# Writing the high and the low parts of three mixed weights in one operation each, in a Strassen-style fp32 matrix product

## The reference, cut to what matters

```python
for i in range(DEPTH):                      # DEPTH = 2
    x = x + token_mixer_i(_rmsnorm(x, g_i)) # attention, then short convolution
    x = x + _swiglu(_rmsnorm(x, f_i), w_gate[i], w_up[i], w_down[i])

def _swiglu(h, w_gate, w_up, w_down):
    return (jax.nn.silu(h @ w_gate) * (h @ w_up)) @ w_down
```

## Time and profile before

| what | value |
| --- | --- |
| time, median of 3 runs | 2097.96 us (2097.86 to 2098.32) |
| span of the profiled execution, first to last instruction | 2096.4 us |
| mean granted TensorE clock over the span | 0.999 of full speed |
| busy: TensorE matmul / weight load / DVE / ACT / POOL | 2081.3 / 1729.7 / 1725.3 / 1177.2 / 118.3 us |
| read from HBM | 429.12 MB, 206 GB/s over the span |

### The profile page before, as it was taken

One profiled execution on the slowest core, in us unless ns is written; L12 is line 12 of the kernel. 1 busy time (PEld: TensorE's weight loads), 2 busy tenths in 40 slices (PEclk: granted clock), 3 DMA queues, 4 the chain that ended last, 5 costly groups with the idle time before them and its releaser, 6 DMA issues.

```text
span 2096.4 us, 28772 instructions
## 1 busy us (share of the span) xinstructions
PE 2081.3 (99%) x9675; PEld 1729.7 (83%) x9675; DVE 1725.3 (82%) x1968; ACT 1177.2 (56%) x1428; POOL 118.3 (6%) x131
## 2 busy tenths in 40 slices
PE   8999999999999999999999999999999999999999
PEld 7888878788888888888888888888888888888887
DVE  5887757999999997876788877579999999978666
ACT  5456555665566564554465555466655665645443
POOL 0001000001000000000000000000010000000000
PEclk9999999999999999999999999999999999999999
DMA  7555456777777777667667666567777777767674
GB/s 230 152 145 152 158 171 192 223 224 227 228 226 220 231 219 215 216 202 215 211 196 211 204 203 196 190 196 222 224 226 229 225 221 230 221 213 216 204 220 147
DMA packets 251616, 432.33 MB, mean 206 GB/s; under 512 B 16912, under 2 KB 58000, under 8 KB 251536
## 3 DMA queue, kind: packets, MB, share of 16 engines
q1 hardware_dynamic: 233824, 399.23, 58.8%
q0 software_dynamic: 16848, 30.68, 8.7%
q10 hardware_dynamic: 864, 1.37, 0.2%
HBM read 429.12 MB, written 2.10 MB: 206 GB/s over the span
## 4 chain that ended last, share of the span: by engine, by line
PE 96%; DVE 2%; ACT 1%; issue 1%; DMA 0%; ACTq 0%; DVEq 0%; SPq 0%
PE ps L774 24%; PE ps L776 24%; PE ps L775 24%; PE ps L520 6%; PE ps L551 4%; PE ps L549 4%; PE ps L550 4%; PE ps L525 3%; PE ps L584 2%; DVE w_lo L1393 1%; PE ps L702 0%; PE ps L640 0%; ACT w_hi L1006 0%; PE ps L711 0%; PE ps L692 0%
## 5 line engine op out<-in xcount | busy, mean ns | idle before, releaser
L1393 DVE TENSOR_TENSOR w_lo<-stage,w_hi 128x1024 fp32r<-128x1024 f32 x748 | 902.3, 1222 | 232.4 <-ACT w_hi L1006 228.4
L1006 ACT ACTIVATE w_hi<-stage 128x1024 fp32r<-128x1024 f32 x748 | 772.7, 1055 | 536.6 <-PE ps L776 365.5
L774 PE MATMUL ps<-w_hi,xs 128*128 128x512 f32 x1122 | 439.4, 392 | 0.3
L776 PE MATMUL ps<-w_hi,xs 128*128 128x512 f32 x1122 | 437.0, 389 | 0.0
L775 PE MATMUL ps<-w_lo,xs 128*128 128x512 f32 x1122 | 436.6, 389 | 0.0
L774 PEld LDWEIGHTS ps<-w_hi,xs 128*128 128x128 f32 x1122 | 210.6, 188 | 44.3 <-DVE gated L1699 1.1
L776 PEld LDWEIGHTS ps<-w_hi,xs 128*128 128x128 f32 x1122 | 210.6, 188 | 44.1
L775 PEld LDWEIGHTS ps<-w_lo,xs 128*128 128x128 f32 x1122 | 210.7, 188 | 42.9
L774 PE MATMUL ps<-w_hi,hs 128*128 128x512 f32 x584 | 227.6, 390 | 0.0
L776 PE MATMUL ps<-w_hi,hs 128*128 128x512 f32 x584 | 227.2, 389 | 0.0
L775 PE MATMUL ps<-w_lo,hs 128*128 128x512 f32 x584 | 227.2, 389 | 0.0
(11 more groups left out here) (226 smaller groups left out, 2824.7 us busy)
## 6 DMA issues: line engine op xcount, KB each, us to landing
stage<-in_w_gate SPq DMA_DIRECT2D x176, 512.0 KB, 4.0
stage<-in_w_up SPq DMA_DIRECT2D x176, 512.0 KB, 4.9
stage<-in_w_down SPq DMA_DIRECT2D x176, 512.0 KB, 4.9
stage<-in_conv_w_in SPq DMA_DIRECT2D x96, 512.0 KB, 4.8
stage<-in_attn_w_in SPq DMA_DIRECT2D x48, 512.0 KB, 3.8
stage<-in_w_gate POOLq DMA_DIRECT2D x86, 256.0 KB, 5.6
stage<-in_attn_w_out SPq DMA_DIRECT2D x32, 512.0 KB, 4.8
stage<-in_conv_w_out SPq DMA_DIRECT2D x32, 512.0 KB, 4.8
```

The costliest lines, as they stand in the source:

```text
L774: pe.matmul(ps[:, bank, :], hi, b_hi, start=start, stop=False)
L776: return pe.matmul(ps[:, bank, :], lo, b_hi, start=False, stop=stop)
L1006: nc.scalar.activation(w_hi[:, j % RING, :], stage[:, at, :], ACT.Copy).then_inc(hi_done, 1)
L1393: tt(w_lo[:, p, :], stage[:, stage_at(first + j), :], f32(w_hi[:, p, :]), ALU.subtract).then_inc(lo_done, 1)
```

## The change

ACT writes the high parts of all three mixed weights in one operation of 1536 elements a partition, and DVE writes their low parts in one. Both `t_high` and `t_ready` rise once for a mixed pair instead of twice. TensorE waits for `t_ready` once, ahead of P6. ACT's early wait (for `t_raw[2]` and for P6 of the pair before) is gone, and only the wait for all of `t_raw` and for P7 of the pair before is left. The other waits on `t_ready` are counted anew and mean what they meant.

```diff
@@ mixed_pair, on TensorE
-                pe.wait_ge(t_ready, 2 * (count + s) + 1)
+                pe.wait_ge(t_ready, count + s + 1)
                 product(P6, mixed_operand(kp, s, 1), t_hi[:, 2, :], t_lo[:, 2, :], first, last).then_inc(t_used, 1)
-                pe.wait_ge(t_ready, 2 * (count + s) + 2)
                 product(P4, half(operand, k2, 1), t_hi[:, 1, :], t_lo[:, 1, :], False, False)
                 product(P7, mixed_operand(kp, s, 3), t_hi[:, 0, :], t_lo[:, 0, :], first, last).then_inc(t_used, 1)
@@ mixed_high, on ACT
-                act.wait_ge(t_step, 2 * count + 1)
-                if not isinstance(count, int) or count:
-                    act.wait_ge(t_used, 2 * count - 1)
-                nc.scalar.activation(t_hi[:, 2, :], t_raw[:, 2, :], ACT.Copy).then_inc(t_high, 1)
                 act.wait_ge(t_step, 2 * count + 2)
                 if not isinstance(count, int) or count:
                     act.wait_ge(t_used, 2 * count)
-                nc.scalar.activation(t_hi[:, 0:2, :], t_raw[:, 0:2, :], ACT.Copy).then_inc(t_high, 1)
+                nc.scalar.activation(t_hi[:, :, :], t_raw[:, :, :], ACT.Copy).then_inc(t_high, 1)
@@ mixed_low, on DVE
-                dve.wait_ge(t_high, 2 * count + 1)
-                tt(t_lo[:, 2, :], t_raw[:, 2, :], f32(t_hi[:, 2, :]), ALU.subtract).then_inc(t_ready, 1)
-                dve.wait_ge(t_high, 2 * count + 2)
-                tt(t_lo[:, 0:2, :], t_raw[:, 0:2, :], f32(t_hi[:, 0:2, :]), ALU.subtract).then_inc(t_ready, 1)
+                dve.wait_ge(t_high, count + 1)
+                tt(t_lo[:, :, :], t_raw[:, :, :], f32(t_hi[:, :, :]), ALU.subtract).then_inc(t_ready, 1)
@@ take_p1 on ACT, mix_x and mix_weights on DVE: the same waits, counted by one a pair
-                act.wait_ge(t_ready, 2 * (count + len(mixed_pairs)))
+                act.wait_ge(t_ready, count + len(mixed_pairs))
-                    dve.wait_ge(t_ready, 2 * (LAYER_MIXED * (q // 2) + 2))
+                    dve.wait_ge(t_ready, LAYER_MIXED * (q // 2) + 2)
-                    dve.wait_ge(t_ready, 2 * count)
+                    dve.wait_ge(t_ready, count)
```

## The result

| | before | after |
| --- | --- | --- |
| median of the runs shown | 2098.0 us (4 runs) | 2141.8 us (2141.1 to 2142.0, 4 runs) |
| span of the profiled execution | 2096.4 us | 2140.4 us |

The ratio is 1.0207, with a 95% interval from 1.0193 to 1.0222. The change makes the kernel slower by 43.8 us. The forecast was 2139.6, with a range from 2129 to 2151.

The account below looks back on a forecast made before the run. TensorE was taken to set the end, so late t_lo is lost whole: 37.6 us in 38 following pairs, 3.6 in first blocks, 0.4 in block 10, sum 41.6. On the median 2097.96 that makes 2139.6 us, range 2129 to 2151.

Parts of the forecast that it names:

- What bounds the kernel: Whole span: TensorE sets the end; delays where it never waits are lost whole, savings elsewhere return some 3 us at most.
- The chain and its price: Pairs following another: ACT's start to P6's load takes 3.35 us against 2.24 available; P6 1.11 us late, net 0.99.
- the 41.6 us of the sum: Both networks: 37.6 us from 38 following pairs, 3.6 from the first blocks, 0.4 from pair 2 of block 10.
- The first blocks: Block 0, twice: DVE sets the pace; pairs 3, 5 and 6 lose 0.97, 0.39 and 0.45, 1.81 us a block.
- What was costed at nothing: Middle blocks' pairs 2 and 5, down projections, convolution: t_lo in time, no loss; DVE's saved fixed cost also counted as nothing.
- no queue loses ground against TensorE: Behind the stalls in following pairs: DVE, ACT, SP and POOL move by no more than TensorE, so the loss doesn't grow.
- A: Rival, whole span: saved fixed cost relieves DVE and ACT, TensorE's waits on DVE shrink, 2094.8 us; 2 in 100.
- 0.07 us a pair: All mixed pairs: DVE time saved by merging, the fixed part of one operation less its overlap; costed at nothing.
- B: Rival, following pairs: no change, P6 isn't held or ACT starts 1.1 us sooner, 2098 plus or minus 2; 4 in 100.
- C: Rival, following pairs: merged operations cost as much as two apart, 1.70 and 1.91 us, total 2155; 5 in 100.
- D: Rival, both networks: new gaps drop the clock to its lower level, 45 to 90 us more, 2185 to 2230; 2 in 100.

Follow-up runs that it names:

- e1: Kernel before, but TensorE waits once, ahead of P6, for both low parts; ACT and DVE keep two operations each: 2104.5 us, ratio 1.0029.
- e2: Kernel before, but ACT writes the high parts in one operation; DVE keeps two operations and TensorE two waits: 2125.0 us, ratio 1.0127.
- e3: Kernel before, but DVE writes the low parts in one operation and TensorE waits once; ACT keeps two operations: 2122.1 us, ratio 1.0114.
- e4: Changed kernel, but undone in the 42 mixed pairs that follow another at once; the 75 others stay merged: 2099.8 us, ratio 1.0008.
- e10: Changed kernel, but only the 42 mixed pairs that follow another at once are merged, the 75 others undone: 2144.1 us, ratio 1.0215.
- e8: Kernel before, but in pairs following another, P6, P4, P7 come behind the next slot's first 6 matmuls, that slot split first: 2101.0 us, ratio 1.0013.
- e5: Changed kernel, but in pairs following another, P6, P4, P7 come behind the next slot's first 6 matmuls, that slot split first: 2104.2 us, ratio 1.0031.
- e9: Changed kernel, but pairs 6 as in the kernel before, and pairs 3 with P6, P4, P7 behind the next slot's first 6 matmuls: 2101.1 us, ratio 1.0015.
- e11: Changed kernel, but ACT's merged operation raises t_high by two and DVE waits for both raises: 2141.4 us, ratio 1.0211.
- e12: Changed kernel, but ACT's merged operation raises t_high by two and DVE waits for the first raise only: 2142.2 us, ratio 1.0213.

## Why the prediction was right

**What bounds the kernel.** Right. TensorE had no wait in the middle blocks, and each new wait is in the time: 44 waits with 48.1 us in all, and 42.7 us more from the mark to the end.

**The chain and its price.** Right, and now measured apart. 3.33 us from ACT's start to P6's load, where 3.35 was worked out. e1, e2 and e3 show its parts: 0.43 us more of ACT, 0.54 more of DVE, and the place of the wait, which alone would cost 6 us of the 43. e4 and e10 show that it does so in the neighbours only.

**The terms.** Beside the 41.6 us of the sum stand 42.7 from the mark on. A stall of 1.09 gives back some 0.12 at the next load (0.11 in place of 0.227), and the matmuls behind it run a little wider (0.23 apart in place of 0.227) for some time, so the net is 1.02, not 0.99: 38 x 0.03 = 1.1 us. The first blocks were put at 1.81 each. By the shift of their loads against the kernel before they cost 1.74 and 1.76. The median lies 43.8 above. The span of the profiled execution lies 44.0 above, and 1.3 of that arose before the mark, in code that is the same. So some 1 us of the distance between 2139.6 and 2141.8 isn't the change's as far as the profiled executions tell.

**What was costed at nothing.** Right for the change: pairs 2 and 5 of the middle blocks, the down projections and the convolution have no wait for `t_lo`. The seven waits of 0.15 us for a slot's low part behind pair 2 weren't foreseen, and cost next to nothing. But one check was missing. I said that no queue loses ground against TensorE, and looked at slot 14 and at SP and POOL, not at the gate bank, which has a spare of 0.16 us. Here it held, because TensorE is delayed as much as DVE (the spare is 0.22 us after). In e2 it cost some 8 us.

**The rivals.** A (the saved fixed cost helps): TensorE's waits on low parts didn't shrink, and DVE's busy time didn't fall by the 0.07 us a pair, 8 us in all, that the prediction gave it (1725.3 us before, 1725.8 after). The busy time of the page is the time in which an engine has some instruction running, and not the sum of their lengths, as the section on the time before has it: 9675 matmuls of 389 ns would sum to more than the span. The sum of DVE's lengths did fall, by 117 x (0.685 + 1.221 - 1.759) = 17 us, so the operations overlap less than before. Why isn't shown. Of the Trainium skill's two rules (Perfetto Trace Analysis, Optimizing Scalar/DVE Operations), grouping for a saturated engine gave nothing here at a busy share of 94.5%. The other, to break up what holds another engine, is stated for engines that aren't saturated; here it held at 94.5% too, with 48.1 us of new waits on TensorE for the merged result. B and C fall with the trace, and e10's 1.23 us waits are the nearest to C. D: the granted clock is 1.00 in the window with 18 new gaps of 1.1 us.

No version here beats the kernel before. It leaves 3 us of waits in its two first blocks, and e8, which was to win part of them, lost more at the bank.

## What to carry to other kernels

Price a merge by dates, not by busy time. Where an engine can't start a write until the last reader is done, the first small part is what the reader gets early, and a merged operation hands it over at the date of the last: here 1.0 us each time, for an estimated 0.07 us saved on an engine that TensorE waited for in two blocks only. The chain was tight only where the buffer is used twice in quick succession, so look for the pairs that differ (42 of 117) before multiplying. And when an edit delays one engine more than the one that sets the end, look for the next handover between the two and its spare: with only 0.16 us to spare at the gate bank, e2 lost 27 us where the chain gave 19.

## What was not expected of the hardware

- The start of the same program varies: the first transposes of the residual stand at 287.9 to 290.9 us in the profiled executions of these kernels, whose code up to there is the same. The transposes of the last quarter of x already differ, from 17.3 us (e5) over 19.1 (before) to 20.3 (after). A pair of matmuls of 512 and 256 columns takes 0.64 us from 13.7 us on in the kernel before, and 0.35 from about 17 on; after, the slow pace lasts to about 18 us; in e5 it is 0.35 from 13.3 us on. In the kernel before, the granted clock is 0.50 of full speed from 14 to 16 us, the lower of the two levels (1.2 GHz), and 1.00 from 18 us on; TensorE had stood idle for 2.4 us ahead of 12.4 us, as it did after and in e5 too. So there the slow stretch is the clock's. In the kernel after, the profile shows 1.00 through the same slow pace, so its clock there isn't shown. This spread is as large as the smaller effects here.
- In e4, e9 and e10 the DVE operation that raises its semaphore by two started 0.07 us later behind ACT than the merged one of the changed kernel, which raises by one. e11 and e12 show that ACT's raise by two isn't the cause, and the cause is open.
- Behind each of the 44 waits for `t_lo` TensorE's second weight load follows at 0.10 to 0.12 us in place of 0.227, so a stall gives back some 0.12 us at once. The next eight loads then follow at 0.231, and 0.08 us is left of it at slot 14.
